# Delta-rule stage of a one-core block: three engines' work put in another order

## What is computed

```python
proj = u @ w_in                                   # 1024 -> q, k (8 heads x 128), v, z (16 x 128), b, a (16)
qkv = jax.nn.silu(causal_dwconv(proj[..., :GDN_QKV_DIM], conv_w))       # 4 taps over positions
q = jnp.repeat(l2_norm(q) * (GDN_HEAD_K ** -0.5), rep, axis=2)
k = jnp.repeat(l2_norm(k), rep, axis=2)
beta = jax.nn.sigmoid(b.astype(jnp.float32))
g = -jnp.exp(a_log) * jax.nn.softplus(a + dt_bias)
# S_t = a_t (I - b_t k_t k_t^T) S_{t-1} + b_t k_t v_t^T,  o_t = S_t^T q_t, in chunks:
m = jnp.where(strict, beta[..., :, None] * kk * decay, 0.0)
a = m + jnp.eye(C)
sol = lax.linalg.triangular_solve(a, rhs, left_side=True, lower=True, unit_diagonal=True)
o = rms_norm(o, norm_gain) * jax.nn.silu(z)
return o.reshape(B, S, GDN_VAL_DIM) @ w_out
```

## Time and profile before

| | us |
|---|---|
| runs, median of 3 | 1781.95 (1778.39 to 1782.19) |
| profiled execution | 1779.81 |
| its span in the trace | 1778.0 |
| PE busy in the span | 1734.3 (98%) |
| DVE busy | 1419.0 (80%) |
| ACT busy | 1011.8 (57%) |
| of it, the stage: turn-in, turns 0, 1, 2, and turn 3 | 51.3, 62.5, 62.1, 65.3, 58.4 |

### The profile page before, as it was taken

The page is one execution under the profiler, slowest core; times in us unless marked ns, Lnnn a source line. Parts: engine busy times, 40 slices in busy tenths (PEclk is TensorE's granted clock), DMA queues, the critical chain, the costliest instruction groups (busy, mean ns, idle before and its releaser), DMA issues.

```text
span 1778.0 us, 32327 instructions
## 1 busy us (share of the span) xinstructions
PE 1734.3 (98%) x12926; PEld 1547.9 (87%) x12926; DVE 1419.0 (80%) x2433; ACT 1011.8 (57%) x1680; POOL 85.3 (5%) x163
## 2 busy tenths in 40 slices
PE   7999999999999999999999999999999999999998
PEld 6888888888888898889888888888898889988887
DVE  4758889788877588888988877898989898867664
ACT  3657764666765577655655322655556555566553
POOL 0000001000000000000001100010101010000000
PEclk9999999999999999999999999999999999999999
DMA  5256559443332356568788833788978787536552
GB/s 197 88 186 201 190 187 347 143 144 131 112 117 85 120 202 212 189 238 313 280 284 293 322 133 105 281 309 283 322 252 315 275 319 266 164 130 205 189 190 95
DMA packets 102819, 373.90 MB, mean 210 GB/s; under 512 B 11440, under 2 KB 11600, under 8 KB 102544
## 3 DMA queue, kind: packets, MB, share of 16 engines
q1 hardware_dynamic: 80352, 289.77, 46.5%
q0 software_dynamic: 22320, 82.09, 13.6%
HBM read 370.74 MB, written 1.08 MB: 209 GB/s over the span
## 4 chain that ended last, share of the span: by engine, by line
PE 83%; DVE 8%; ACT 4%; issue 2%; DMA 2%; DVEq 0%; SPq 0%; ACTq 0%
PE ps L650 36%; PE ps L653 20%; PE ps L657 2%; DVE weights_lo L618 2%; PE ps L658 2%; PE ps L659 2%; PE ps L1074 2%; PE ps L748 2%; PE ps L1259 1%; PE ps L2369 1%; ACT weights_hi L611 1%; DMA ffn_tiles<-in_ada 1%; DVE arena L2488 1%; PE ps L2395 1%; DVE u L2045 1%
## 5 line engine op out<-in xcount | busy, mean ns | idle before, releaser
L618 DVE TENSOR_TENSOR weights_lo<-weight_ring,weights_hi 128x1024 fp32r<-128x1024 f32 x493 | 601.5, 1222 | 129.4 <-ACT weights_hi L611 128.9
L611 ACT ACTIVATE weights_hi<-weight_ring 128x1024 fp32r<-128x1024 f32 x493 | 518.1, 1057 | 159.5 <-PE ps L650 104.8
L650 PE MATMUL ps<-u_halves,weights_hi 128*128 128x512 f32 x2048 | 495.0, 391 | 0.9 <-DVE u_halves L473 0.5
L650 PEld LDWEIGHTS ps<-u_halves,weights_hi 128*128 128x128 f32 x2048 | 376.3, 188 | 75.8 <-DVE weights_lo L618 1.0
L653 PEld LDWEIGHTS ps<-u_halves,weights_lo 128*128 128x128 f32 x2048 | 266.0, 191 | 10.4 <-DVE weights_lo L618 0.3
L653 PE MATMUL ps<-u_halves,weights_lo 128*128 128x256 f32 x2048 | 274.2, 283 | 0.2
L650 PE MATMUL ps<-act_halves,weights_hi 128*128 128x512 f32 x952 | 231.6, 391 | 0.1
L650 PEld LDWEIGHTS ps<-act_halves,weights_hi 128*128 128x128 f32 x952 | 173.4, 188 | 33.0 <-DVE weights_lo L618 0.5
L887 DVE SCALAR_TENSOR_TENSOR ffn_tiles<-ffn_tiles,cond 128x1024 f32<-128x1024 f32 x144 | 175.3, 1219 | 5.3 <-DMA ffn_tiles<-in_ada 5.1
L780 ACT ACTIVATE ffn_tiles<-ps 128x512 f32<-128x512 f32 x128 | 76.0, 594 | 143.9 <-PE ps L653 143.7
L657 PE MATMUL ps<-u_halves,weights_hi 128*128 128x256 f32 x456 | 137.8, 302 | 16.0 <-DVE u L2045 12.7
(11 more groups left out here) (346 smaller groups left out, 2342.9 us busy)
## 6 DMA issues: line engine op xcount, KB each, us to landing
weight_ring<-in_w SPq DMA_DIRECT2D x545, 512.0 KB, 3.9
ffn_tiles<-in_ada POOLq DMA_DIRECT2D x144, 512.0 KB, 5.4
scaled<-gates_scratch POOLq DMA_DIRECT2D x8, 512.0 KB, 5.4
arena<-in_alibi POOLq DMA_DIRECT2D x1, 1536.0 KB, 6.8
h<-in_x SPq DMA_DIRECT2D x4, 256.0 KB, 3.6
out<-u SPq DMA_DIRECT2D x4, 256.0 KB, 2.1
consts<-in_consts SPq DMA_DIRECT2D x1, 592.0 KB, 9.5
cond<-in_cond SPq DMA_DIRECT2D x1, 512.0 KB, 10.3
```

The costliest lines, as they stand in the source:

```text
L611: nc.scalar.activation(w_slot(s)[0], ring[:, n % RING], ACT.Copy).then_inc(hi_ready, 1)
L618: nc.vector.tensor_tensor(lo, ring[:, n % RING], hi.bitcast(F32), ALU.subtract).then_inc(lo_ready, 1)
L650: return nc.tensor.matmul(ps[:, bank], hi, halves, start=start, stop=stop, skip_group_check=True)
```

## The change

1. **Slots.** In the stage, unit 2 of turn 0 gets a fourth slot, and the units behind it rotate over three as before but one place on, so that the splits of the units 2 to 5 wait for a unit that is done one unit earlier.
2. **Turn-in.** ACT splits unit 2 first of all. Beta is 1 / (1 + exp(-b)): ACT's Sigmoid, with a table load of its own, goes, and DVE adds 1 and takes a reciprocal. `gates_dve` has the same number of instructions, and stands behind unit 3's taps instead of unit 1's; PE's `gate_cols_pe` stands behind unit 6 instead of unit 4.
3. **Turn 0's levels 0 to 3** put their first products into banks 2 and 3, so that they no longer wait for all masked products; the second part of those (`masked_second_dve`) moves behind level 0 on DVE.
4. **Level 3 in one piece.** ACT first copies the whole 128x128 result (`g_x32`), then the three pieces to `x64`; DVE turns it with one instruction for each t; ACT copies four diagonal pieces for each t to `xt_` (`diagonal_act`), and level 4's second product waits for those (`g_diag`).
5. **Orders.** DVE's and ACT's lists of a turn are dealt anew: taps earlier against the levels, `out_root_act` behind the first tap and split, `mix_dve` behind level 1, `qk_norm_dve` behind unit 6's split, `mix_lo_dve` behind level 5, and unit 2's low half of the next turn moved into that turn.
6. **PE**: unit 9's first half stands between `first_values` and `v_turn`.

```diff
-                gdn_out = n - FIRST_UNIT["gdn_out"]
+                gdn_in, gdn_out = n - FIRST_UNIT["gdn_in"], n - FIRST_UNIT["gdn_out"]
+                if 2 <= gdn_in and gdn_out < 0:
+                    s = 3 if gdn_in == 2 else gdn_in % GDN_SPLIT
                 if gdn_out == 0:
                     used[3] = FIRST_UNIT["gdn_in"] + 12 * (GH // GB) - 3
...
 
             if lv < SMALL:
-                return {"p": 4, "xi": 6}[which] + t
+                return {"p": 4 if i else 2, "xi": 6}[which] + t
...
                         pe.wait_ge(g_vb, 2)
-                if 0 < lv <= SMALL:
+                if 0 < lv < SMALL:
                     pe.wait_ge(g_xb, blocks_until(i, lv - 1, t))
+                if lv == SMALL:
+                    pe.wait_ge(g_diag, 2 * i + t + 1)
                 if lv < LEVELS - 1:
...
             first_values_pe(pe, i)
+            gdn_unit_pe(pe, n, 9, (0,))
             v_turn_pe(pe, n)
             cross_pe(pe, i)
             kk_pe(pe, n)
-            gdn_unit_pe(pe, n, 9)
+            gdn_unit_pe(pe, n, 9, (1,))
...
-            nc.scalar.activation(gates[0:16], ps[0:16, 4, 0:T], ACT.Sigmoid).then_inc(g_beta, 1)
+            nc.scalar.activation(tb_[0:16], ps[0:16, 4, 0:T], ACT.Exp, scale=-1.0).then_inc(g_beta_exp, 1)
...
+                bank = level_bank(i, lv, "xi", t)
                 if lv < SMALL - 1:
                     last = nc.scalar.activation(flat(x_[:, t]), ps[:, bank, 0:GB * Q], ACT.Copy)
                 elif lv == SMALL - 1:
-                    for r in QUARTERS[0], HALVES[1]:
+                    nc.scalar.activation(flat(x_[:, t]), ps[:, bank, 0:GB * Q], ACT.Copy).then_inc(g_x32, 1)
+                    if i == 0 and t == 0:
+                        act.wait_ge(g_cleared, 2)
+                    for r in QUARTERS[0], QUARTERS[2]:
                         nc.scalar.activation(x64[r, t, :, 0:Q], heads(r, bank), ACT.Copy)
                     r = QUARTERS[1]
...
+        def diagonal_act(act, i, t):
+
+            act.wait_ge(g_xb, blocks_until(i, SMALL - 1, t))
+            for r in QUARTERS:
+                last = nc.scalar.activation(xt_[r, i % 2, t, :, r], xb[r, t], ACT.Copy)
+            last.then_inc(g_diag, 1)
...
             dve.wait_ge(g_soft, 2)
-            m(nc.vector.tensor_scalar(tb_[a], xa[a], 0.0, None, ALU.max))
-            m(nc.vector.tensor_scalar(nea[a], nea[a], -1.0, None, ALU.mult))
+            m(nc.vector.scalar_tensor_tensor(tb_[a], xa[a], 0.0, ta[a], ALU.max, ALU.add))
+            dve.wait_ge(g_beta_exp, 1)
+            m(nc.vector.tensor_scalar(tb_[0:16], tb_[0:16], 1.0, None, ALU.add))
+            w(1)
+            at, _ = CONST["reset"]
+            m(nc.vector.tensor_tensor_scan(ta[a], consts[a, at:at + T], tb_[a], 0.0, ALU.mult, ALU.add))
+            w(1)
+            nc.vector.reciprocal(gates[0:16], tb_[0:16]).then_inc(g_beta, 1)
             w()
-            m(nc.vector.tensor_tensor(tb_[a], tb_[a], ta[a], ALU.add))
-            w()
-            m(nc.vector.tensor_scalar(tb_[a], tb_[a], nea[a], None, ALU.mult))
-            w()
-            at, _ = CONST["reset"]
-            nc.vector.tensor_tensor_scan(gates[a], consts[a, at:at + T], tb_[a], 0.0, ALU.mult, ALU.add).then_inc(g_gates, 1)
+            nc.vector.tensor_scalar(gates[a], ta[a], nea[a], -1.0, ALU.mult, ALU.mult).then_inc(g_gates, 1)
 
         def gate_cols_dve(dve, steps):
...
             for t in range(2):
-                if i == 0 and lv == SMALL - 1 and t == 0:
-                    dve.wait_ge(g_cleared, 2)
-                dve.wait_ge(g_x, 2 * (LEVELS - 1) * i + 2 * lv + t + 1)
                 if lv < SMALL - 1:
-                    last = nc.vector.transpose(flat(xb[:, t]), flat(x_[:, t]))
+                    dve.wait_ge(g_x, 2 * (LEVELS - 1) * i + 2 * lv + t + 1)
                 else:
-                    for n, r in enumerate(QUARTERS):
-                        at = Q if n == 1 else 0
-                        last = nc.vector.transpose(xt_[r, i % 2, t, :, r], x64[r, t, :, at:at + Q])
+                    dve.wait_ge(g_x32, 2 * i + t + 1)
+                last = nc.vector.transpose(flat(xb[:, t]), flat(x_[:, t]))
                 last.then_inc(g_xb, 1)
 
...
             gdn_clear_dve(dve)
-            taps_conv_dve(dve, steps, 0, 0)
             split_lo(dve, "gdn_in", 2)
-            taps_conv_dve(dve, steps, 0, 1)
-            gdn_lo_dve(dve, 0, 0)
+            for j in range(4):
+                taps_conv_dve(dve, steps, 0, j)
+                if j < 3:
+                    gdn_lo_dve(dve, 0, j)
             gates_dve(dve, steps)
-            gdn_lo_dve(dve, 0, 1)
-            for j in range(2, 5):
-                taps_conv_dve(dve, steps, 0, j)
-                gdn_lo_dve(dve, 0, j)
+            gdn_lo_dve(dve, 0, 3)
+            taps_conv_dve(dve, steps, 0, 4)
+            gdn_lo_dve(dve, 0, 4)
+            taps_conv_dve(dve, steps, 0, 5)
             gate_cols_dve(dve, steps)
-            taps_conv_dve(dve, steps, 0, 5)
...
             level_dve(dve, i, 0)
+            if i == 0:
+                masked_second_dve(dve, steps, 0)
+                turn_blocks_dve(dve, i, 0)
             decay_args_dve(dve, steps, n, 0)
-            turn_blocks_dve(dve, i, 0)
             decay_args_dve(dve, steps, n, 1)
             if i:
+                turn_blocks_dve(dve, i, 0)
+            gdn_lo_dve(dve, i, 11)
+            taps_conv_dve(dve, steps, n, 0)
+
+            level_dve(dve, i, 1)
+            gdn_lo_dve(dve, n, 0)
+            taps_conv_dve(dve, steps, n, 1)
+            turn_blocks_dve(dve, i, 1)
+            if i:
                 mix_dve(dve, i - 1)
-
-            level_dve(dve, i, 1)
-            taps_conv_dve(dve, steps, n, 0)
-            turn_blocks_dve(dve, i, 1)
-            taps_conv_dve(dve, steps, n, 1)
-            gdn_lo_dve(dve, n, 0)
+            gdn_lo_dve(dve, n, 1)
 
             level_dve(dve, i, 2)
-            gdn_lo_dve(dve, n, 1)
+            taps_conv_dve(dve, steps, n, 2)
             turn_blocks_dve(dve, i, 2)
-            taps_conv_dve(dve, steps, n, 2)
             gdn_lo_dve(dve, n, 2)
+            taps_conv_dve(dve, steps, n, 3)
+
+            level_dve(dve, i, 3)
+            gdn_lo_dve(dve, n, 3)
+            taps_conv_dve(dve, steps, n, 4)
+            turn_blocks_dve(dve, i, 3)
+
+            level_dve(dve, i, 4)
```

More of the change, by code:

```diff
@@ L1405, in lower_until, with level_bank @@
             return 2 * (LEVELS - SMALL) * i + 2 * (lv - SMALL) + t + 1
-        def level_bank(lv, which, t):
+        def level_bank(i, lv, which, t):
             if lv < SMALL:
-                return {"p": 4, "xi": 6}[which] + t
+                return {"p": 4 if i else 2, "xi": 6}[which] + t
             a = 4 + 2 * (lv % 2)
@@ L1518, in level_first_pe @@
                     pe.wait_ge(g_x0, 2 * i + t + 1)
-                    if t == 0:
+                    if i == 0 and t == 1:
+                        pe.wait_ge(g_masked, 1)
+                    if i and t == 0:
                         pe.wait_ge(g_masked, 2 * i + 2)
                 else:
+                    if lv == SMALL and t == 0:
+                        pe.wait_ge(g_masked, 2 * i + 2)
                     pe.wait_ge(g_x, 2 * (LEVELS - 1) * i + 2 * (lv - 1) + t + 1)
@@ L1654, in gdn_pe @@
             gdn_unit_pe(pe, 0, 6)
+            gate_cols_pe(pe)
             gdn_unit_pe(pe, 0, 7)
@@ L1743, in gdn_gates_act, with gdn_softplus_end_act @@
             m(nc.scalar.activation(nea[a], cols[a, COL["a_log"]:COL["a_log"] + 1], ACT.Exp))
-            w()
+        def gdn_softplus_end_act(act, steps):
+            steps.wait()
+            a = slice(32, 48)
             nc.scalar.activation(ta[a], ta[a], ACT.Ln, bias=cols[a, COL["one"]:COL["one"] + 1]).then_inc(g_soft, 1)
-        def gdn_beta_act(act):
-            nc.scalar.activation(gates[0:16], ps[0:16, 4, 0:T], ACT.Sigmoid).then_inc(g_beta, 1)
+            nc.scalar.activation(tb_[0:16], ps[0:16, 4, 0:T], ACT.Exp, scale=-1.0).then_inc(g_beta_exp, 1)
         def gdn_hi_act(act, i, j):
@@ L1845, in level_chunk_act @@
             act.wait_ge(g_ix, lower_until(i, lv, t))
-            bank = level_bank(lv, "ix", t)
+            bank = level_bank(i, lv, "ix", t)
             if lv == SMALL:
@@ L1879, in gdn_act @@
         def gdn_act(act, steps):
+            split_hi(act, "gdn_in", 2)
             tap_act(act, 0, 0)
-            split_hi(act, "gdn_in", 2)
-            gdn_gates_act(act, steps)
+            gdn_hi_act(act, 0, 0)
+            gdn_softplus_act(act, steps)
             tap_act(act, 0, 1)
-            gdn_hi_act(act, 0, 0)
-            gdn_beta_act(act)
+            gdn_softplus_end_act(act, steps)
+            gdn_hi_act(act, 0, 1)
+            tap_act(act, 0, 2)
+            gdn_hi_act(act, 0, 2)
             silu_conv_act(act, 0, 0)
-            gdn_hi_act(act, 0, 1)
-            for j in (2, 3):
-                tap_act(act, 0, j)
-                silu_conv_act(act, 0, j - 1)
-                gdn_hi_act(act, 0, j)
```

(39 more changed lines are left out.)

57 lines of the change are left out of this document (27 added, 30 removed).

## The result

The changed kernel takes 1761.37 us (median of four runs, 1760.25 to 1762.71) against 1782.07 of the kernel before in the same measurement: a ratio of 0.9886, with a 95% interval from 0.9866 to 0.9905. That is 20.7 us less; 1766 was forecast, with a range of 1758 to 1776. The profiled execution has a span of 1758.7 us, 19.3 less than before.

A forecast was written before the change was run, and what follows sets the result against it. PE, busy 98%, was taken to bound the kernel, its waits on DVE and low clock the stage's loss. 1.5 + 3.65 + 6.8 + 2.6 = 14.5 off 1779.81 gave 1765.3, rounded up to 1766, range 1758 to 1776.

The forecast's parts named there:

- Who bounds the stage: Stage: PE is busy 98%; its 19.6 us idle and 6.8 of clock, 26 us, are the most to gain.
- as walked: Whole kernel: the terms come out as summed, 1766 us, own range 1761 to 1770; chance 0.62.
- the gates are no loss: Turn-in and turn 0: units 3 us earlier, reciprocal 0.34, rows land by 351, turn 0 gains 5: 1762; chance 0.11.
- signs named for the first case: Stage: tap waits under 3 us, turns 1 and 2 at 58 to 60, clock 1.00, only long PE idle ahead of kk.
- Turn 1: Turn 1: waits for taps go, leaving only PE's work, 62.10 - 58.45 = 3.65 us gained.
- turn 2: Turn 2: 3.40 us idle and the 3.4 of clock behind its wait go, 6.8 gained.
- The example of unit 6: PE's wait for unit 4's taps: taps ahead of DVE's transposes remove the 2.23 us wait, with 2.7 to spare.
- Turn 3: Turn 3: mix_lo_dve ends 1.7 us earlier, half the clock's loss goes: 2.6 gained (1.7 to 3.9).
- Turn-in and turn 0: Turn-in and turn 0: later gates and rows delay DVE, earlier units and fewer waits outweigh it: 1.5 us gained.
- The way through DRAM: Turn-in and turn 0: g's and beta's rows land 11.0 us behind the gates' end, and decay_args_dve waits for them.
- The reciprocal: DVE's 16x256 reciprocal for beta in the gates: 1.4 us, bounds 0.34 and 2.5; 2.7 if eight times a plain instruction.
- ACT's diagonal copies: Ahead of level 4's second product: slack about 0.8 us, costed at nothing; as slower rival 1787, chance 0.05.

The follow-up runs named there:

- shortest stage of any run: Changed kernel with g's rows stored and loaded without beta, and turn 0's decay_args of the next turn behind level 1's mask: 1755.7 us (0.9851).
- run with slow diagonal copies: Changed kernel with each of ACT's diagonal copies cut into four, one for each head: 1772.07 us (0.9935).
- two runs with half of the change: Kernel before with level 3 in one piece alone: 1768.3 us (0.992); changed kernel with level 3 as before: 1766.45 us (0.991).
- run with eight transposes: Changed kernel with level 3 as before (three copies, eight transposes, no diagonal copies): 1766.45 us (0.991).
- run with g's rows first: Changed kernel with g's rows stored and loaded without beta, the reciprocal behind unit 4's taps: 1756.71 us (0.9849).

## Why the prediction was right

**Who bounds the stage** held: what PE stood idle and the low clock were put at 26 us as the most that could be won, and 18.0 came. The shortest stage of any run (290.3) is 24.1 below the kernel before, still inside.

**The time** fell inside the range, but the sum was too small. The terms made 14.5; the stage gave 18.0, the profiled span 19.3, and the medians 20.7. Three of the four terms below were put too low, so 1761.37 stands at the lower edge of the range of the case *as walked* (1761 to 1770) and is nearest to the 1762 of the case *the gates are no loss*. That case's mechanism is not what happened: the reciprocal took 1.74 and not 0.34, and `decay_args_dve` waited for the rows until 352.98, not 351. The signs named for the first case did come: one wait for taps of 1.1, turns of 57.95 and 59.05 at a clock of 1.00, and the one long wait ahead of kk.

**Turn 1** was put at 3.65 and measured 4.15; **turn 2** at 6.8 and 6.25, with 0.9 of PE's time in it that the profile marks "issue". Both turns lost all their waits for data, and turn 2's clock stayed at 1.00. PE's busy time itself fell by 0.5 in turn 1 (58.45 to 57.95), which I hadn't expected: the length less the busy time isn't quite all that waits cost. The run with slow diagonal copies shows the same from the other side: one wait of 1.18 in turn 1, and a turn 1.73 longer.

**The example of unit 6** held. In turn 1 unit 4's taps now end at 455.98, ahead of the transposes, and PE starts unit 6 at 458.21 without a wait, 2.2 us later, where 2.7 were forecast (rows of DVE's and PE's timelines):

```profile
454.46 1.52 DVE L2070 SCALAR_TENSOR_TENSOR u<-ps,cols,u 128x253 f32<-128x253 f32 x3 [0.67 <-ACT u L1779]
```

```profile
458.21 0.39 PE L659 MATMUL ps<-u_halves,weights_hi 128*128 128x256 f32 x1
```

But its reading was one-sided. I gave the wait to the order on DVE; the two runs with half of the change show that shorter transposes remove almost all of it as well, and that for this wait, in turns 0 to 2, either is enough.

**Turn 3** was mis-sized: 2.6 forecast (1.7 to 3.9), 4.6 measured, above its range. `mix_lo_dve` came early enough that 0.3 of the wait of 2.24 was left, a little better than the 0.5 of the forecast; the clock's loss went whole, where I had taken half; and the "issue" waits of the profile before in that stretch (0.7 and 0.4) weren't there, which no run of mine explains. That the wait and the clock hang together is shown by the run with eight transposes, which brought back both (2.26, clock 0.66). "Only the transposes change here" was not quite so: a split (1.22) also moved into DVE's list of this turn. The run with eight transposes has it too, so it doesn't explain the gain.

**Turn-in and turn 0** were put at a gain of 1.5, and gave 3.0 (113.8 to 110.8). The chain was as described: gates, rows, `decay_args_dve`, kk, with half clock around PE's idle time of 3.96 ("some 5" forecast). Since the stage itself began 0.7 us earlier in the trace after, I count its sizes from the stage's first product (323.27 and 322.61):

- The gates' end: 20.0 forecast, 20.5 measured. That is near by two terms set against each other and never summed, the units' earlier start ("1 to 3") and the reciprocal. In the run with g's rows first, which has no reciprocal ahead of g, g ends at 18.7: the units came 1.3 earlier, and the reciprocal took 1.74 back.
- The way through DRAM: I took the 11.0 of before, it was 9.9. The 1.1 is the landing of the second load, 6.6 us in place of 7.7. (The 348.8 of the forecast is that load's issue, 341.1, and 7.7; with the 1.09 that the text names it would be 349.3.)
- `decay_args_dve`: 31.0 forecast, 30.4 measured.
- Level 1's second product in turn 0: 62.2 forecast, 61.2 measured, behind a wait of 0.95 for the mask. From there to turn 1: 50.0 forecast, 49.6 measured.

So the term that was off is the way through DRAM, and part of it was made up by the gates' end.

**The reciprocal** took 1.74 where I had 1.4: with the fixed 166 ns that is 6.2 ns an element, nine times the 0.69 of a plain instruction. The Trainium skill ("VectorE: DVE Perf Modes", section "First, the fixed hardware budget") states a repeat count of 8 for the divide. Taken as a factor of eight on the elements alone, which is an estimate, that gives 8 x 0.69 ns x 256 + 0.17 = 1.6 us, near the measured time; on the whole instruction, as I had applied it (2.7), it was too much.

**ACT's diagonal copies** had a slack of 0.8 by the walk and about 1.0 by experiment; "costed at nothing" was right, and not by much. **Unit 9's half** has no term in the prediction at all, though without it the turns 0 to 2 wait 3.2 us for a SiLU: that the terms of these turns came out rests on a cover that the prediction didn't price.

What no run took apart: turn 0's levels in other banks, and how much each move in the lists contributes. The fourth slot's share isn't clear of the scatter. The three "issue" waits stay unexplained.
